# Odd layer of a hybrid decoder trunk: gate products of a block parted, gate projections moved, output tiles paired

## What is computed

```
def causal_conv(x, buf, w, bias): ...          # 4 taps along the sequence
def rg_lru(x, h0, w_r, b_r, w_i, b_i, lam):
    xb = x.reshape(bsz, slen, LRU_BLOCKS, LRU_BLOCK)
    r = sigmoid(einsum('bsnc,ncd->bsnd', xb, w_r) + b_r)
    i = sigmoid(einsum('bsnc,ncd->bsnd', xb, w_i) + b_i)
    log_a = -LRU_C * r * softplus(-lam)
    a = exp(log_a)
    b = sqrt(-expm1(2.0 * log_a)) * (i * x)
    ...                                        # h[t] = a[t] * h[t-1] + b[t]
def odd_mixer(x, ...):
    p = rmsnorm(x, g_norm) @ w_in
    gate = gelu(p[..., :LRU_WIDTH])
    xc, conv_new = causal_conv(p[..., LRU_WIDTH:], s_conv, conv_w, conv_b)
    h, lru_new = rg_lru(xc, s_lru, w_r, b_r, w_i, b_i, lam)
    mix = (gate * h) @ w_out
```

## Time and profile before

| what | value |
|---|---|
| median of 3 runs | 2349.11 us (2340.26 to 2349.56) |
| profiled execution, its own time | 2353.24 us |
| its span, first to last instruction | 2351.4 us |
| mean granted TensorE clock | 0.983 of full |
| PE busy / PEld busy | 2281.7 us (97%) / 2212.8 us (94%) |
| DVE / ACT busy | 1197.8 us (51%) / 647.3 us (28%) |
| chain that ended last, by engine | PE 89%, DVE 6%, ACT 3% |

### The profile page before, as it was taken

The page is one execution under the profiler, slowest core; times in us unless marked ns, Lnnn a source line. Parts: engine busy times, 40 slices in busy tenths (PEclk is TensorE's granted clock), DMA queues, the critical chain, the costliest instruction groups (busy, mean ns, idle before and its releaser), DMA issues.

```text
span 2351.4 us, 32438 instructions
## 1 busy us (share of the span) xinstructions
PE 2281.7 (97%) x13986; PEld 2212.8 (94%) x13986; DVE 1197.8 (51%) x1331; ACT 647.3 (28%) x700; POOL 23.1 (1%) x39
## 2 busy tenths in 40 slices
PE   7999989999999999999999998999999999999997
PEld 7988679899999999999999887999999999999996
DVE  8776557464334434443448766544443443444344
ACT  5223532342111111111115545333112111111113
POOL 0000000000000000000000000000000000000001
PEclk9999979799999999999999999999999999999999
DMA  4334213331111111111111111111111111111102
GB/s 167 108 103 122 94 62 106 119 116 44 54 45 45 36 54 45 45 53 45 37 44 48 41 41 47 42 45 45 37 54 45 45 45 44 45 45 54 45 27 74
DMA packets 59257, 141.69 MB, mean 60 GB/s; under 512 B 6368, under 2 KB 30512, under 8 KB 59184
## 3 DMA queue, kind: packets, MB, share of 16 engines
q1 hardware_dynamic: 52848, 122.84, 15.5%
q0 software_dynamic: 3888, 14.16, 1.8%
q10 hardware_dynamic: 2448, 3.64, 0.4%
HBM read 121.08 MB, written 19.53 MB: 60 GB/s over the span
## 4 chain that ended last, share of the span: by engine, by line
PE 89%; DVE 6%; ACT 3%; issue 1%; DMA 1%; SPq 0%; ACTq 0%; DVEq 0%; POOLq 0%
PE acc L546 83%; PE ms L546 2%; DVE TT L1481 1%; PE acc L768 1%; ACT TT L1146 0%; DVE XP L1481 0%; DVE XL L1484 0%; ACT L1146 0%; DVE WL L1481 0%; PE acc L847 0%; DMA y_scratch<-G 0%; PE acc L783 0%; DMA WR<-in_w_stream 0%; DMA VH<-y_scratch 0%; PE ms L599 0%
## 5 line engine op out<-in xcount | busy, mean ns | idle before, releaser
L546 PE MATMUL acc<-XH,WH 128*128 128x352 f32 x2608 | 857.3, 329 | 37.7 <-ACT TT L1146 14.1
L546 PE MATMUL acc<-XH,WL 128*128 128x352 f32 x2608 | 844.7, 324 | 0.0
L546 PE MATMUL acc<-XL,WH 128*128 128x352 f32 x2608 | 842.5, 323 | 0.0
L546 PEld LDWEIGHTS acc<-XH,WH 128*128 128x128 f32 x2608 | 493.9, 189 | 50.2 <-issue 32.6
L1481 DVE TENSOR_TENSOR X<-X,acc 128x1056 f32<-128x1056 f32 (+1 forms) x288 | 343.2, 1193 | 386.2 <-PE acc L546 386.2
L546 PE MATMUL acc<-HH,WH 128*128 128x352 f32 x1536 | 496.6, 323 | 1.4 <-DVE X L1481 1.4
L546 PEld LDWEIGHTS acc<-XL,WH 128*128 128x128 f32 x2608 | 497.0, 191 | 0.0
L546 PE MATMUL acc<-HH,WL 128*128 128x352 f32 x1536 | 495.9, 323 | 0.0
L546 PE MATMUL acc<-HL,WH 128*128 128x352 f32 x1536 | 495.3, 322 | 0.0
L546 PEld LDWEIGHTS acc<-XH,WL 128*128 128x128 f32 x2608 | 493.7, 189 | 0.0
L1037 ACT ACTIVATE WH<-WR 128x1024 fp32r<-128x1024 f32 x179 | 184.9, 1049 | 619.7 <-PE acc L546 554.1
(11 more groups left out here) (308 smaller groups left out, 1358.3 us busy)
## 6 DMA issues: line engine op xcount, KB each, us to landing
WR<-in_w_stream SPq DMA_DIRECT2D x152, 512.0 KB, 3.2
WR<-in_w_stream POOLq DMA_DIRECT2D x27, 512.0 KB, 4.1
X<-in_x_t SPq DMA_DIRECT2D x8, 528.0 KB, 10.2
LA<-in_x_t SPq DMA_DIRECT2D x24, 176.0 KB, 2.5
xz_scratch<-LA SPq DMA_DIRECT2D x24, 176.0 KB, 1.8
X<-xz_scratch SPq DMA_DIRECT2D x8, 528.0 KB, 5.5
out_y_t<-X SPq DMA_DIRECT2D x12, 352.0 KB, 2.4
u_scratch<-UR SPq DMA_DIRECT2D x4, 576.0 KB, 3.0
```

The costliest lines, as they stand in the source:

```text
L546: return pe.matmul(out, lhs, rhs, start=start, stop=stop)
```

## The change

On TensorE a block is now r n, gate n-1, i n, xb n+2 (block 0: r0, xb2, i0; block 6: r6, gate5, i6). Then follow gate6, r7, i7, gate7. The output tiles outo0 and outo1 are made as a pair, and `project_pair` claims each buffer only where its first matmul goes there. On ScalarE, `gates` is parted into `decays_of` (sigmoid of r, tanh, exp, sqrt) and `inputs_of` (sigmoid of i, after the gelu and the weight copy). Block 7 has an order of its own there, with r7 kept in XP and the copies of the mix set between its activations. On VectorE, `take_gate` is parted from the multiply (`use_gate`), gets a wait for the exp of the next block (which reads TT[0]), and moves ahead of the recurrence, which takes the multiply by i later; in block 7 the recurrence stands between the low parts of the mix.

```diff
 _odd = ["xb0", "xb1"]
 for _n in range(KT):
-    _odd += [f"r{_n}", f"i{_n}"] + ([f"gate{_n - 1}"] if _n else []) + ([f"xb{_n + 2}"] if _n + 2 < KT else [])
-_odd.append(f"gate{KT - 1}")
+    if _n < KT - 1:
+        _odd += [f"r{_n}", f"gate{_n - 1}" if _n else "xb2", f"i{_n}"] + ([f"xb{_n + 2}"] if 0 < _n < KT - 2 else [])
+_odd += [f"gate{KT - 2}", f"r{KT - 1}", f"i{KT - 1}", f"gate{KT - 1}"]
...
             def project_pair(names, acc_names, xn):
-                claim(t)
-                claim(t + 1)
                 for k in range(KT):
                     pe.wait_ge(xl_done, xn + k + 1)
                     for j in range(2):
                         if k == 0:
+                            claim(t + j)
                             split_wait(pe, n + j)
...
-            for n in range(KT):
-                gates(n)
+            for n in range(KT - 1):
+                gate_of(n, 0)
                 if n:
                     project(f"gate{n - 1}", f"gate{n - 1}")
-                if n + 2 < KT:
+                else:
+                    project("xb2", "xb2")
+                gate_of(n, 1)
+                if 0 < n < KT - 2:
                     project(f"xb{n + 2}", f"xb{n + 2}")
+            project(f"gate{KT - 2}", f"gate{KT - 2}")
+            gate_of(KT - 1, 0)
+            gate_of(KT - 1, 1)
             project(f"gate{KT - 1}", f"gate{KT - 1}", free=True)
-            for m in range(KT):
-                project(f"outo{m}", f"outo{m}", xn=SPLIT["mix"] if m == 0 else None, free=(m == KT - 1))
+            project_pair(("outo0", "outo1"), ("outo0", "outo1"), SPLIT["mix"])
+            for m in range(2, KT):
+                project(f"outo{m}", f"outo{m}", free=(m == KT - 1))
...
-            def gates(n):
-                if n:
-                    act.wait_ge(states_done, n)
+            def decays_of(n):
+                if n == 1:
+                    act.wait_ge(gates_done, 3)
                 if n >= 2:
                     act.wait_ge(hb_ready, n - 1)
                 read_plain(f"r{n}", TT[:, 0, :], ACT.Sigmoid, bias=p_col("b_r", n))
-                read_plain(f"i{n}", TT[:, 1, :], ACT.Sigmoid, bias=p_col("b_i", n))
                 read_wait(act, f"r{n}")
+                if n:
+                    act.wait_ge(states_done, n)
...
+            def inputs_of(n):
+                t = ACC[f"i{n}"]
+                done_wait(act, f"i{n}")
+                act.activation(cut(TT[:, 1, :]), bank(t), ACT.Sigmoid, bias=p_col("b_i", n)).then_inc(acc_read[t % 2], 1)
...
-            for n in range(KT):
-                gates(n)
-                if n + 2 < KT:
-                    load_ri(n + 2)
+            for n in range(KT - 1):
+                decays_of(n)
                 if n:
                     gelu_gate(n - 1)
                     hi(STREAM[f"gate{n - 1}"] + SLOTS)
+                inputs_of(n)
                 if n + 2 < KT:
+                    load_ri(n + 2)
+                if n < KT - 2:
                     read_wait(act, f"xb{n + 2}")
                     hi(STREAM[f"xb{n + 2}"] + SLOTS)
...
+            gelu_gate(KT - 2)
+            hi(STREAM[f"gate{KT - 2}"] + SLOTS)
+            n = KT - 1
+            act.wait_ge(conv_done, KT)
+            read_plain(f"r{n}", XP[:, 0:T], ACT.Sigmoid, bias=p_col("b_r", n))
+            act.wait_ge(states_done, n)
+            inputs_of(n)
+            read_wait(act, f"r{n}")
+            act.activation(TT[:, 3, :], XP[:, 0:T], ACT.Tanh, scale=sp4[:, n:n + 1]).then_inc(gates_done, 1)
+            free_hi(0)
+            act.activation(TT[:, 2, :], XP[:, 0:T], ACT.Exp, scale=sp8[:, n:n + 1]).then_inc(gates_done, 1)
+            free_hi(1)
+            act.wait_ge(gates_done, 3 * n + 1)
+            act.activation(TT[:, 3, :], TT[:, 3, :], ACT.Sqrt).then_inc(gates_done, 1)
+            for k in range(2, KT - 1):
+                free_hi(k)
+            gelu_gate(n)
+            hi(STREAM[f"gate{n}"] + SLOTS)
+            mix_hi(n)
...
             def recur(n):
-                dve.wait_ge(gates_done, 3 * n + 1)
-                link(tt(TT[:, 1, :], TT[:, 1, :], HB[:, n, :], ALU.mult))
                 dve.wait_ge(gates_done, 3 * n + 3)
                 link(stt(TT[:, 3, :], TT[:, 2, :], 1.0, TT[:, 3, :], ALU.add, ALU.mult))
+                read_wait(dve, f"i{n}")
+                link(tt(TT[:, 1, :], TT[:, 1, :], HB[:, n, :], ALU.mult))
...
                 done_wait(dve, f"gate{m}")
+                dve.wait_ge(gates_done, 3 * min(m + 1, KT - 2) + 2)
                 tt(cut(TT[:, 0, :]), bank(t), cut(RS[:, :]), ALU.mult).then_inc(acc_read[t % 2], 1)
+            def use_gate(m):
                 dve.wait_ge(gelu_done, m + 1)
                 tt(HB[:, m, :], HB[:, m, :], TT[:, 0, :], ALU.mult).then_inc(hb_ready, 1)
...
-            for n in range(KT):
-                recur(n)
-                if n:
-                    take_gate(n - 1)
-                    lo_w(STREAM[f"gate{n - 1}"] + SLOTS)
-                if n + 2 < KT:
+            take_xb(2)
+            recur(0)
+            conv(2)
+            lo_w(STREAM["xb2"] + SLOTS)
+            for n in range(1, KT - 1):
+                take_gate(n - 1)
+                use_gate(n - 1)
+                lo_w(STREAM[f"gate{n - 1}"] + SLOTS)
+                recur(n)
+                if n < KT - 2:
                     take_xb(n + 2)
                     conv(n + 2)
                     lo_w(STREAM[f"xb{n + 2}"] + SLOTS)
-            for k in range(KT - 1):
-                mix_lo(k)
+            take_gate(KT - 2)
+            use_gate(KT - 2)
+            lo_w(STREAM[f"gate{KT - 2}"] + SLOTS)
+            mix_lo(0)
+            mix_lo(1)
+            dve.wait_ge(hb_ready, KT - 1)
             take_gate(KT - 1)
+            mix_lo(2)
+            mix_lo(3)
+            recur(KT - 1)
+            mix_lo(4)
+            use_gate(KT - 1)
+            mix_lo(5)
+            mix_lo(6)
             lo_w(STREAM[f"gate{KT - 1}"] + SLOTS)
             mix_lo(KT - 1)
```

More of the change, by code:

```diff
@@ L967, in _, with gate_of @@
             mlp(0, 1)
-            def gates(n):
[L971 to L978, removed]
+            def gate_of(n, r):
+                name = "ri"[r]
+                t = ACC[f"{name}{n}"]
+                if r == 0:
+                    pe.wait_ge(conv_done, n + 1)
+                    pe.wait_ge(wri_in[n % 2], 16 * (n // 2 + 1))
+                claim(t)
+                for c in range(NCH):
+                    last = mm(acc[:, t % 2, c, 0:CH], WRI[:, n % 2, r, :], HB[:, n, c * CH:(c + 1) * CH], True, True)
+                last.then_inc(acc_done[t % 2], 1)
             project("xb0", "xb0", xn=SPLIT["norm2"])
@@ L1456, in _, with free_hi @@
                     hi(STREAM[f"gate{n - 1}"] + SLOTS)
+                inputs_of(n)
                 if n + 2 < KT:
+                    load_ri(n + 2)
+                if n < KT - 2:
                     read_wait(act, f"xb{n + 2}")
                     hi(STREAM[f"xb{n + 2}"] + SLOTS)
-            for k in range(KT - 1):
+            def free_hi(k):
                 act.wait_ge(x_free, 3 + k + 1)
                 mix_hi(k)
-            gelu_gate(KT - 1)
-            hi(STREAM[f"gate{KT - 1}"] + SLOTS)
-            mix_hi(KT - 1)
+            gelu_gate(KT - 2)
[17 more added lines that the diff above has]
+            mix_hi(n)
             act.wait_ge(states_done, KT)
@@ L2220, in _ @@
                     lo_w(STREAM[f"xb{n + 2}"] + SLOTS)
-            for k in range(KT - 1):
-                mix_lo(k)
-            take_gate(KT - 1)
+            take_gate(KT - 2)
[4 more added lines that the diff above has]
+            dve.wait_ge(hb_ready, KT - 1)
+            take_gate(KT - 1)
+            mix_lo(2)
[5 more added lines that the diff above has]
+            mix_lo(6)
             lo_w(STREAM[f"gate{KT - 1}"] + SLOTS)
```

## The result

The median went from 2347.77 us (8 runs, 2340.26 to 2350.84) to 2335.91 us (8 runs, 2331.99 to 2337.25). The ratio is 0.9948 with a 95% interval of 0.9934 to 0.9962, that is 9 to 15.5 us saved. The forecast was 2336.1 us.

The account below looks back on a forecast made before the run. TensorE, at work 97% of the span, bounds the kernel, losing 14.1 us in eight waits for ScalarE. Terms 11.8 + 1.0 + 0.8 + 0.6 - 0.5 - 0.7 = 13.0 us off 2349.1 give 2336.1, range 2327 to 2346.

Parts of the forecast that it names:

- Blocks 0 to 6 and the first blocks: Parted products save 11.8 us over seven blocks, block 1's wait 1.0; VectorE's late first gate eviction and start lose 0.5.
- the two passages from product to projection: In each block, TensorE loses 0.08 us whenever a projection follows a product; parting the products adds one such passage.
- The spare of 1.4 us on VectorE: Per block, VectorE's queue from gate tile to next xb tile takes 12.0 us against 13.4 on TensorE.
- the rival in which the wait moves to the evictions: Evictions of xb and gate come 0.4 us later at thirteen places, costing 5 us: 2341 us; chance 0.18.
- the forecast's 0.8 + 0.6: Last block: 0.8 us from the 0.61 us wait going, 0.6 from the wait ahead of gate7 shrinking.
- the 1.4 us of drain: At the last wait, a table switch would add some 1.38 us by the skill's rule; the forecast left it out.
- the same fall: Behind the 2.4 us wait ahead of gate7 the clock falls as before, at 2.8 us: no gain.
- the rival in which the clock holds: 2.4 us idle ahead of gate7 is too little to lower the clock: 15.8 us saved, 2333.3 us; chance 0.27.
- The pair: Making outo0 and outo1 together loses 0.7 us (between 0 and 2), waiting for VectorE's fifth operand split.
- The slower rival: A lone product between projections lowers the clock in every block, 2.8 us per fall: 2355.7 us; chance 0.05.

Follow-up runs that it names:

- the added multiplies: The changed kernel with three extra VectorE multiplies (3.87 us) ahead of the recurrence in blocks 1 to 6: stretch xb0 to outo2 265.1 us, against 244.8.
- one multiply more: The changed kernel with one extra VectorE multiply (1.29 us) ahead of the recurrence in blocks 1 to 6: stretch xb0 to outo2 244.4 us, against 244.8.
- the run with the sigmoid first: The changed kernel with ScalarE's sigmoids of r7 and i7 and the tanh ahead of gate6's gelu: stretch 241.2 us against 244.8, median 2332.97 us.
- the one with the old blocks: The changed kernel with blocks 0 to 6 back to r, i, gate, xb, sigmoids together, the new end kept: stretch 258.2 us, against 244.8.
- the pair alone: The kernel before with only the outo0/outo1 pair and the later claim of each buffer: stretch 258.6 us, as before.
- the kernel with all three: The changed kernel with block 7's sigmoids first, xb2's weight split behind the first gate eviction, block 7's recurrence behind the fifth low part: stretch 239.1 us, against 244.8.

## Why the prediction was right

**Blocks 0 to 6 and the first blocks.** Forecast 11.8 + 1.0 - 0.5 = 12.3 us. From the start of r0 to the end of the same fourteen products and twelve projections, TensorE takes 176.8 us before (1283.66 to 1460.44) and 164.9 after (1281.58 to 1446.46): 11.9. The end of before, 1460.44, stands in the earlier trace rows; the other three rows are these, the first from before:

```profile
1283.66 3.94 PE L546 MATMUL acc<-HB,WRI 128*128 128x352 f32 x12
...
1281.58 1.94 PE L547 MATMUL acc<-HB,WRI 128*128 128x352 f32 x6
...
1446.46 0.49 PE L547 MATMUL acc<-XH,WH 128*128 128x352 f32 x1
```

The blocks from r2, r3 and r4 take 26.77, 26.62 and 26.64 us against a forecast of 26.65; the one from r5 takes 27.08, for it has a wait, and that is about what is missing from the 12.3. The wait at the start is 0.56 where 0.4 was expected. One term was wrong in its parts and right in sum: the two passages from product to projection cost 0.19 us a block, where 0.08 each were taken. Six small matmuls are 0.296 us apart, and those of a projection 0.16. After r3's last the projection starts 0.41 us later and its second matmul 0.24 after its first, 0.19 in all; after i3's last the projection starts 0.13 us later and its second matmul follows 0.33 after, which comes to nothing.

**What hides the work.** The spare of 1.4 us on VectorE was 1.52 as idle time and 1.53 by the added multiplies. Apart from the wait of 0.56 us in block 1, for the eviction of gate0, which the forecast had, the evictions of gate and xb stay off the path in all blocks but one. Block 5 has 0.32 us ahead of gate4, where the eviction of xb6 began 0.64 us after the start of the product instead of 0.27:

```profile
1404.29 1.94 PE L547 MATMUL acc<-HB,WRI 128*128 128x352 f32 x6
1406.55 0.40 PE L547 MATMUL acc<-XH,WH 128*128 128x352 f32 x1 [0.32 <-DVE XP L1516]
...
1404.93 0.18 DVE L2187 COPY XP<-st_conv 128x24 f32<-128x24 f32 x1 [1.89 <-PE acc L547]
```

So the rival in which the wait moves to the evictions holds in one place of thirteen, and not for want of time on VectorE, which had been idle for 1.89 us; with one multiply more the wait was not there. What held the eviction stays open.

**The end.** From behind block 6 to gate7's start 21.9 us became 17.8, 4.1 less, of which 2.7 are the half clock that gate6 no longer sees (14.4 us before, 11.6 after); the rest, 1.4, is the forecast's 0.8 + 0.6. The wait is 2.46 us against 2.4, and the run with the sigmoid first shows that it is ScalarE's queue: without gelu, copy and table load ahead it goes. The table load is again followed by its activation at once (1461.67 + 1.28, 1462.96), so the 1.4 us of drain that the Trainium skill (ScalarE: Activation LUTs, What ACT_TABLE_LOAD costs) would add was rightly left out.

**The clock.** Here a term was mis-sized. I had written: "2.4 us is nearer to 2.96, so I take the same fall: no gain." It fell, but for less. The engines in stretches of the tile behind the wait (columns as above), before and then after:

```profile
1468.00:1473.50 5.50, 5.50 (x19) 5.50 (x20) 1.26 (x1) 5.45 (x5) 0.00 (x0) 0.50 0.22 86
1474.50:1482.00 7.50, 7.50 (x48) 7.50 (x47) 5.51 (x8) 1.61 (x2) 0.00 (x0) 1.00 0.00 0
...
1465.00:1468.00 3.00, 3.00 (x12) 3.00 (x11) 0.22 (x1) 2.52 (x4) 0.00 (x0) 0.50 0.28 105
1469.00:1477.00 8.00, 8.00 (x52) 8.00 (x51) 1.30 (x2) 7.96 (x9) 0.00 (x0) 1.00 0.00 0
```

Half clock, 1.2 GHz, held for at least 5.5 us before, and after for at least 3.0 but under 5, for it is full from 1469 us on. So gate7 took 13.1 us where it took 11.6 before, 1.5 lost, against the 2.7 that gate6 had lost: a gain of 1.3 us that the forecast had put at nothing. The result lies between the forecast and the rival in which the clock holds. Nor is the step from the idle time to the fall sound: 2.46 us let the clock fall in four of the five kernels that have it and not in the one with the old blocks, and 2.96 us let it fall in the kernel before and not with the pair alone. Of the fourteen waits of 2.3 to 3.0 us in these ten traces' stretches, ten have a fall behind them. A wait in this range makes a fall likely, and its length does not decide it.

**The pair.** outo0 and outo1 take 23.9 us together where they took 23.2: 0.7 lost, as forecast, but not by the forecast's parts. The fifth low part costs 0.6 us (0.6 to 0.7 were forecast), of which only 0.3 show as idle time; the kernel with all three, without that wait, takes 23.3 us here. Besides, the holds by the evictions of gate7 and, at outo2, of outo0 cost 0.2 each (0.1 for the first alone was forecast), and 0.3 come back because the matmuls of these tiles are 0.159 us apart and no longer 0.161 (last section). That the term comes out is in part luck.

Sum of the stretch: 11.9 + 4.1 - 1.5 - 0.7 = 13.8, against 13.0; the terms that differ are the blocks (0.4 less) and the clock (1.3 more). The median moved by 11.9, and both sums lie in its interval of 9 to 15.5. That the median itself came within 0.2 us of 2336.1 is luck: with more runs the kernel before has a median 1.3 us lower than the one that the forecast started from, and the saving by medians is 1.1 under the forecast. The saving of 16.9 between the two profiled executions holds 2.1 from ahead of the odd layer and is no measure of the change. The slower rival, a clock that falls at each lone product, is out: the clock is 1.00 from 1290 to 1450 us.

## What to carry to other kernels

When two short products hold both output buffers of an engine, put a long tile between them: the read-out of each then lies under a tile instead of between tiles. What decides such a reordering is the slack of the engines that now release the buffers; work it out per period before, and check it by adding a known amount of work, which is free up to the slack and paid in full beyond it. Where one wait is left at the end of a pipeline, look at what is queued ahead of the releasing instruction on its engine rather than at that instruction.

## What had not been expected

A wait of TensorE can cost more than its length: behind waits of 2.3 to 3.0 us the granted clock went from 2.4 to 1.2 GHz in ten cases of fourteen, and each of these falls cost 1.5 to 2.8 us on the next tile. In the kernel with three more multiplies four such falls cost 6.3 us, on top of 13.8 us of waits for evictions. What decides whether it falls, and for how long, is not shown.

The tiles outo2 to outo7 take 11.60 us each in the kernel before and 11.44 to 11.52 in all the others, 0.9 us for six tiles with the same matmuls. Two instructions more ahead of outo2 (the extra wait) didn't change it, nor is it the pair (the kernel without it has 11.44 for the tiles behind outo0). With the pair alone, gate7 takes 11.44 us with the same instructions on TensorE ahead of it as in the kernel before, where it takes 11.60 behind a long fall of the clock. What sets it stays open.
